# Up projection of a two-layer encoder step: the order of the token halves in one eighth of a tile

## The reference

```
x = x + rmsnorm(mix, p['norm_mix_post'][i])
h = rmsnorm(x, p['norm_ffn_pre'][i])
f = jnp.square(jax.nn.relu(h @ p['w_up'][i])) @ p['w_down'][i]
x = x + rmsnorm(f, p['norm_ffn_post'][i])
```

## Time and profile before

| | |
|---|---|
| Median of three runs | 1777.16 us |
| Lowest, highest | 1773.88, 1780.49 us |
| Profiled execution, its own time | 1778.79 us |
| Profiled execution, span of the trace | 1777.0 us |
| TensorE busy | 1686.0 us (95%), 12611 matmuls |
| VectorE, ScalarE, GpSimd busy | 1154.2, 835.8, 579.6 us |
| Mean granted TensorE clock | 0.990 |

### The profile page before, as it was taken

How to read it: one execution, slowest core, us unless ns; L and a number is a source line. 1 busy time by engine, 2 the same in 40 slices (tenths; PEclk the granted TensorE clock), 3 DMA queues, 4 the chain that set the end, 5 groups by cost and what they waited for, 6 DMA issues and landing times. The chain is left out here.

```text
span 1777.0 us, 31700 instructions
## 1 busy us (share of the span) xinstructions
PE 1686.0 (95%) x12611; PEld 1611.1 (91%) x12611; DVE 1154.2 (65%) x2100; ACT 835.8 (47%) x1606; POOL 579.6 (33%) x361
## 2 busy tenths in 40 slices
PE   6999999999999999999999999999999999999996
PEld 5987877998999999998899999987998899999996
DVE  6437777315774838477879797967306774838477
ACT  6326666324433434345555666565424534434342
POOL 1231211231443343432125344440341452343431
PEclk9999999999999999999999999999999999999998
DMA  6621111121222322231223223331221222313221
GB/s 227 209 77 55 55 66 31 60 84 48 96 95 72 107 67 101 72 101 54 75 77 105 98 91 94 100 104 61 72 83 40 104 84 83 108 60 108 72 96 54
DMA packets 51491, 153.11 MB, mean 86 GB/s; under 512 B 12400, under 2 KB 14160, under 8 KB 51088
## 3 DMA queue, kind: packets, MB, share of 16 engines
q1 hardware_dynamic: 43968, 139.99, 23.2%
q10 hardware_dynamic: 7376, 11.10, 2.0%
HBM read 144.16 MB, written 6.47 MB: 85 GB/s over the span
## 5 line engine op out<-in xcount | busy, mean ns | idle before, releaser
L1189 PE MATMUL ps<-big_hi,w_hi 128*128 128x288 f32 x2528 | 560.0, 302 | 12.6 <-DVE relu L1969 6.3
L1189 PE MATMUL ps<-big_lo,w_hi 128*128 128x288 f32 x2528 | 541.6, 298 | 7.2 <-DVE big_lo L1666 7.1
L1189 PE MATMUL ps<-big_hi,w_lo 128*128 128x288 f32 x2528 | 545.3, 295 | 0.0
L2412 POOL TENSOR_TENSOR w_lo<-raw,w_hi 128x1024 fp32r<-128x1024 f32 x116 | 284.2, 2451 | 680.2 <-ACT w_hi L611 569.9
L1189 PEld LDWEIGHTS ps<-big_hi,w_hi 128*128 128x128 f32 x2528 | 410.0, 190 | 21.0 <-issue 18.3
L1189 PEld LDWEIGHTS ps<-big_lo,w_hi 128*128 128x128 f32 x2528 | 403.0, 189 | 12.5 <-DVE big_lo L1666 11.6
L1189 PEld LDWEIGHTS ps<-big_hi,w_lo 128*128 128x128 f32 x2528 | 408.4, 189 | 0.1
L1481 PE MATMUL ps<-col_hi,w_hi 128*128 128x288 f32 x896 | 267.5, 299 | 16.9 <-DVE mix L2059 15.8
L1481 PE MATMUL ps<-col_hi,e_lo 128*128 128x288 f32 x896 | 264.4, 295 | 0.0
L1481 PE MATMUL ps<-col_lo,w_hi 128*128 128x288 f32 x896 | 264.0, 295 | 0.0
L611 ACT ACTIVATE w_hi<-raw 128x1024 fp32r<-128x1024 f32 x176 | 185.6, 1055 | 151.3 <-DMA raw<-in_slabs 86.2
(11 more groups left out here) (223 smaller groups left out, 2283.8 us busy)
## 6 DMA issues: line engine op xcount, KB each, us to landing
raw<-in_slabs SPq DMA_DIRECT2D x238, 512.0 KB, 3.3
row<-acs_prompt ACTq DMA_DIRECT2D x16, 384.0 KB, 3.8
bias<-in_alibi SPq DMA_DIRECT2D x12, 256.0 KB, 2.6
x<-in_x SPq DMA_DIRECT2D x2, 1152.0 KB, 8.3
out_h<-state ACTq DMA_DIRECT2D x4, 384.0 KB, 2.6
out_y<-x SPq DMA_DIRECT2D x2, 576.0 KB, 2.8
raw<-in_slabs SPq DMA_DIRECT2D x4, 256.0 KB, 3.7
kms<-in_mk SPq DMA_DIRECT2D x2, 512.0 KB, 5.1
```

What stands on the lines that cost most here:

```text
L1189: ins = pe.matmul(ps[:, bank + h, 0:hi_c - lo_c], weight(w, s, kt), a[:, k0 + kt, lo_c:hi_c], start=start, stop=stop, skip_group_check=True)
L2412: pool.tensor_tensor(w_lo[:, s % RING], raw[:, s % RING], w_hi[:, hi_place(s)].bitcast(F32), ALU.subtract).then_inc(lo_done, 1)
```

## The change

`eighth()` gets an argument `turned`, and `projection()` passes it for kt = 0 only, and only where the MLP loop asks for it: c > 0 and m == 0. There the six matmuls run with the halves in the order 1,0 then 0,1 then 1,0 in place of 0,1 then 1,0 then 0,1. The weights, the products and all waits stay where they are. It concerns six matmuls in each of three chunks in each of two layers, 36 of 12611.

```
-            def eighth(s, g, kt, hi, lo, k0=0, cols=TOK, start=True, stop=True, tile=None):
+            def eighth(s, g, kt, hi, lo, k0=0, cols=TOK, start=True, stop=True, tile=None, turned=False):
                 both = range(2 if cols == TOK else 1)
-                for w, a, order in ((w_hi, hi, both), (w_lo, hi, reversed(both)), (w_hi, lo, both)):
+                if turned:
+                    both = both[::-1]
+                for w, a, order in ((w_hi, hi, both), (w_lo, hi, both[::-1]), (w_hi, lo, both)):
...
-            def projection(k0=KT, hi=big_hi, lo=big_lo, cols=TOK, fresh=False, each=None):
+            def projection(k0=KT, hi=big_hi, lo=big_lo, cols=TOK, fresh=False, each=None, turned=False):
                 begin(n.s, n.g)
                 for kt in range(KT):
-                    eighth(n.s, n.g, kt, hi, lo, k0, cols, tile=n.a + kt if fresh else None)
+                    eighth(n.s, n.g, kt, hi, lo, k0, cols, tile=n.a + kt if fresh else None,
+                           turned=turned and kt == 0)
...
                     for m in range(FRONT if c == 0 else 0, KT):
-                        projection()
+                        projection(turned=c > 0 and m == 0)
```

## The result

The changed kernel takes 1789.92 us in the median of six runs (1784.91 to 1792.15), the kernel before in the same comparison 1778.14 us (1773.88 to 1783.81). The ratio is 1.0059, with a 95% interval from 1.0043 to 1.0074. It is **slower by about 0.6%**, 10.5 us by the ratio. I had forecast 1773.6 us, and the range ended at 1780.5.

The account below looks back on a forecast made before the run. TensorE was taken to bound the kernel. Terms for work, first-tile waits and the six matmuls were 0, the rhythm left behind -3.6 us: from a median of 1777.16 to 1773.6 us, range 1770.3 to 1780.5.

Parts of the forecast that it names:

- TensorE bounds, the seam has no wait, the change adds and removes no work.: Whole kernel and entry to the changed tiles: TensorE busy 1686.0 of 1777.0 us, no wait at L1189, work term 0.
- Starting in the other bank costs nothing.: First tile of the up projection: starting in the other bank meets no reader and adds no wait; term 0.
- The six matmuls themselves: Turned first eighth: pair distances could shift by 0.01 us each, +0.2 to -0.2 us in six tiles; taken as 0.
- What they leave behind.: Up projection's 384 matmuls per chunk: the turned eighth puts TensorE into the faster rhythm, 0.60 us a chunk, -3.6 us in six.
- The bound on the bad side.: Six up-projection stretches: at worst a third, slower rhythm with every pair at 0.27 us, 0.81 us an eighth, +3.8 us.
- Rival B: Second eighth of the six tiles: keeping the half sets off a slower rhythm, up to +3.8 us, 1781.0 us; chance 0.09.
- Rival A: Six up-projection stretches: order has no effect, the stream falls back to 0.80 us an eighth, 1777.2 us; chance 0.36.
- Is the gain kept?: Behind the last tile, VectorE is ready in time, so the gain reaches the down product whole; at most 0.9 us lost.
- The signs to watch for.: Changed stretches, if right: 304 or 305 matmuls in 40 us in place of 302, and 384 matmuls in about 50.6 us.

Follow-up runs that it names:

- banks only: Against the changed kernel, only the banks written are turned in the first eighth, the halves read keep the old order; 51.21 us a stretch of 384 matmuls.
- seam-only kernel: Against the changed kernel, the first eighth's last pair is back in the old order (halves 1,0 0,1 0,1); median 1776.61 us, ratio 0.9989 to the kernel before.

## Why the prediction was wrong, point by point

- **TensorE bounds, the seam has no wait, the change adds and removes no work.** Right. Counts are equal, waits of TensorE in the changed stretch go from 3.4 to 3.5 us, and none stands at L1189.
- **Starting in the other bank costs nothing.** Right, and shown by itself: banks only, 51.21 us.
- **The six matmuls themselves, 0 within 0.2 us.** Right within a hundredth: the turned eighth takes 0.79 us where no more than 0.80 was there before.
- **"What they leave behind."** This is the step that failed. I put it that the disturbed eighth would most likely put TensorE into the faster rhythm, -3.6 us. That the six matmuls choose the rhythm of the 384 was right, and so was that it is then kept. The direction was wrong: the change enters a rhythm of 137.7 ns, 6 x 1.67 = +10.0 us. I had argued "by the nearest row", but the out projection's quick 80 us don't show what this entry does, only that a quick rhythm exists. The chance of 0.55 for the forecast had no more than that behind it.
- **The bound on the bad side.** Rival B named the mechanism and the place (a slower rhythm, set off at the step that keeps the half) but priced it at +3.8 us, by giving every pair the longest pair distance that the trace of before showed. The slow rhythm has pairs of up to 0.28 us and its eighth is 0.826, not 0.81 us. It doesn't occur in a row of before that I read, nor in any unbroken six of these matmuls elsewhere in that trace, so that bound was no bound. The chance of 0.09, the range's end, and the 0.02 for slower by over 0.5%, which is what came, were all too small.
- **Rival A, the order is without effect.** Excluded for the reads, true for the banks and for the weights' order. The Trainium skill (TensorE: Matmul & The Clock Gate, section "Back-to-back issue gap") counts columns and clock in its formula for an isolated matmul, and lets weight load and matmul together set the distance in a stream. Here the same columns and weight loads at a granted clock of 1.00 take 131.7, 133.3 or 137.7 ns, so these alone don't fix it.
- **Is the gain kept?** Right, as the quick kernels show: from one chunk to the next takes 98.50 us before, 97.90 in the seam-only kernel and 1539.01 - 1438.83 = 100.18 in the changed one. What a stretch gains or loses goes through whole.
- **The signs to watch for.** One was miscounted: a quick window of 40 us holds 40 / 0.1317 + 2 = 306 matmuls, as the kernel with the whole first tile turned has from 534 to 574 us, and not 304 or 305. The changed kernel has 293 there.
- **The kernel could have given what I forecast.** One other order of the same six matmuls (1,0 0,1 0,1) goes to 50.59 us a stretch, the 50.6 I had worked out, and so does turning the first four eighths or the whole first tile. My sum was right for the quick rhythm, and the change doesn't reach it.

What stays open is what inside TensorE or its reads makes a rhythm. The runs show that it hangs on the reads of the activations and on what stands ahead of the tile, and not on banks or weight order. They don't show why one and the same program has three steady distances. I didn't separate the address of a half from its being the same as the one read before.

## What to carry to other kernels

Where long runs of equal matmuls bound a kernel, read the distance of their starts, stretch by stretch, and compare stretches of the same code: a difference of one to five per cent with no wait anywhere can be a rhythm set at the entry, as here, and then a handful of matmuls decides the time of all that follow. I found nothing in the trace of before that gives the sign of such an edit; try two or three orders at the entry and look at the length of the stretch in the chain, which here was the same in all six repeats within a kernel, instead of at the total time of a single run. And when a mechanism can end in states that the trace doesn't show, the worst value seen is no bound on it.

## What the runs showed of the hardware that I had not expected

- One program of 128x288 matmuls has three steady distances at the full granted clock: 131.7, 133.3 and 137.7 ns. Behind the same entry all six stretches of a kernel have the same one, in each of the 14 traces.
- Six matmuls with the halves turned can end the middle and the slow rhythm (fifth tile: 6.40 to 6.33 us, 6.62 to 6.32 us a tile). A kept step met in the quick rhythm leaves it as it is (50.59 us a stretch).
- The distance also changes with no edit in or ahead of a stretch. Layer 0's out projection, the same code in all kernels, had 610, 603 and 583 matmuls in 80 us in three executions; of the 14 traces it is quick in eleven, middle in two and slow in one. Between quick and slow lie over 3.6 us, more than half of the 6.6 us by which the first three runs of the kernel before differ, though no trace shows which rhythm those runs had beyond the one that was profiled.
